# First stage of a two-block transformer kernel: x loaded by two queues, the norm's weights loaded as one row and spread by TensorE, one norm chain for all tokens, projection by halves of the contraction

## What is computed

```python
def rmsnorm(x, g):
    xf = x.astype(jnp.float32)
    y = xf * lax.rsqrt(jnp.mean(xf * xf, axis=-1, keepdims=True) + EPS)
    return (y * g.astype(jnp.float32)).astype(x.dtype)

# first_block, cut
n = rmsnorm(h, g_mix[l])          # x: (1, 256, 1024), g_mix: (1, 1024)
proj = n @ w_in[l]                # convolution, queries, three sets of keys and values, gates
# ... convolution mixer, sparse attention with three branches, w_o, residual
# ... rmsnorm with g_ffn, gated feed-forward, residual, rmsnorm with g_final
# second_block: norm, projections, differential attention, gated linear attention,
# pooling, w_out, residual, norm, gated feed-forward, residual
```

## Time and profile before

| | us |
|---|---|
| median of 3 runs (lowest, highest) | 803.18 (801.69, 803.35) |
| the profiled execution | 801.18 |
| its span | 799.4 |
| TensorE matmuls busy in it | 762.5 (95%) |
| VectorE busy | 519.9 (65%) |
| ScalarE busy | 396.4 (50%) |
| GpSimd busy | 74.0 (9%) |

### The profile page before, as it was taken

One profiled execution on the slowest core, in us unless ns is written; L12 is line 12 of the kernel. 1 busy time (PEld: TensorE's weight loads), 2 busy tenths in 40 slices (PEclk: granted clock), 3 DMA queues, 4 the chain that ended last, 5 costly groups with the idle time before them and its releaser, 6 DMA issues.

```text
span 799.4 us, 13826 instructions
## 1 busy us (share of the span) xinstructions
PE 762.5 (95%) x5693; PEld 717.9 (90%) x5693; DVE 519.9 (65%) x886; ACT 396.4 (50%) x711; POOL 74.0 (9%) x106
## 2 busy tenths in 40 slices
PE   2999999999999998999999998998889999999998
PEld 2999999989989988999899987997769999889996
DVE  5666465765655768776456648687887777447662
ACT  5356655455554445455344536468455454444441
POOL 8000000023022001000000003301500000000000
PEclk9999999999999999999999999999999999999999
DMA  9887636234334565565665553643344665665521
GB/s 289 227 263 238 163 69 191 98 107 139 126 107 135 173 193 184 164 207 191 188 199 164 206 182 99 198 143 121 104 144 121 210 209 170 202 209 160 194 72 52
DMA packets 108414, 132.12 MB, mean 165 GB/s; under 512 B 4267, under 2 KB 97513, under 8 KB 108352
## 3 DMA queue, kind: packets, MB, share of 16 engines
q1 hardware_dynamic: 106048, 126.56, 49.7%
q0 software_dynamic: 2304, 4.68, 2.5%
HBM read 129.39 MB, written 1.84 MB: 164 GB/s over the span
## 4 chain that ended last, share of the span: by engine, by line
PE 58%; DVE 7%; ACT 2%; issue 2%; POOL 1%; POOLq 0%; DVEq 0%
PE B L1421 34%; PE B L1438 23%; DVE LO L892 3%; ACT HI L508 1%; POOL SGC L463 1%; DVE AL L898 0%; PE B L1445 0%; PE B L1576 0%; DVE TMP L1337 0%; ACT SGC L820 0%; DVE NW L908 0%; DVE ST L1164 0%; ACT AH L512 0%; DVE SGC L1262 0%; DVE SM L1254 0%
## 5 line engine op out<-in xcount | busy, mean ns | idle before, releaser
L892 DVE TENSOR_TENSOR LO<-RAW,HI 128x1024 fp32r<-128x1024 f32 x240 | 282.5, 1212 | 105.0 <-ACT HI L508 104.5
L1421 PE MATMUL B<-AH,HI 128*128 128x256 f32 x1200 | 345.0, 288 | 5.9 <-DVE SGC L1179 1.9
L1421 PE MATMUL B<-AL,HI 128*128 128x256 f32 x1200 | 340.5, 284 | 0.0
L1421 PE MATMUL B<-AH,LO 128*128 128x256 f32 x1200 | 340.5, 284 | 0.0
L508 ACT ACTIVATE HI<-RAW 128x1024 fp32r<-128x1024 f32 x240 | 237.7, 1039 | 64.1 <-PE B L1438 59.7
L1421 PEld LDWEIGHTS B<-AH,HI 128*128 128x128 f32 x1200 | 230.7, 192 | 8.9 <-DVE SGC L1179 2.3
L1421 PEld LDWEIGHTS B<-AL,HI 128*128 128x128 f32 x1200 | 230.8, 192 | 0.3
L1421 PEld LDWEIGHTS B<-AH,LO 128*128 128x128 f32 x1200 | 230.6, 192 | 0.0
L1438 PE MATMUL B<-HI,AH 128*128 128x512 f32 (+1 forms) x400 | 140.7, 352 | 6.4 <-DVE AL L1353 3.8
L1438 PE MATMUL B<-LO,AH 128*128 128x512 f32 (+1 forms) x400 | 139.4, 348 | 0.0
L1438 PE MATMUL B<-HI,AL 128*128 128x512 f32 (+1 forms) x400 | 139.4, 348 | 0.0
(11 more groups left out here) (274 smaller groups left out, 591.2 us busy)
## 6 DMA issues: line engine op xcount, KB each, us to landing
RAW<-in_w_in SPq DMA_DIRECT2D x30, 1024.0 KB, 5.6
RAW<-in_w_gate SPq DMA_DIRECT2D x22, 1024.0 KB, 5.3
RAW<-in_w_up SPq DMA_DIRECT2D x22, 1024.0 KB, 5.3
RAW<-in_w_down SPq DMA_DIRECT2D x22, 1024.0 KB, 5.0
RAW<-in_w_in SPq DMA_DIRECT2D x9, 512.0 KB, 5.8
RAW<-in_w_attn_out SPq DMA_DIRECT2D x4, 1024.0 KB, 5.1
RAW<-in_w_o SPq DMA_DIRECT2D x4, 1024.0 KB, 5.0
RAW<-in_w_out SPq DMA_DIRECT2D x4, 1024.0 KB, 5.0
```

The lines of the kernel that those rows point to most:

```text
L892: e.tensor_tensor(pieces(LO, NSPL, i, k), pieces(RAW, NRAW, i, k), pieces(HI, NSPL, i, k), ALU.subtract).then_inc(split_lo, 1)
L1421: x = e.matmul(dst, w[:, t, c0:c0 + n], a, start=(t == 0 and k == 0), stop=(t == nk - 1 and k == 2))
```

## The change

- x: SyncE issues the two halves of token tile 0, ScalarE the two halves of token tile 1, each on its own queue.
- Unit 0 is loaded in two halves by chunks (0 to 3, 4 to 7), the first with a semaphore of its own. Behind it, SyncE waits until all of token tile 1 is there before it issues units 1, 2, 3 and so on.
- g_mix is loaded as one row of 4 KB into partition 0. TensorE multiplies it with a row of ones, in two matmuls of 512 columns, which leaves it spread over 128 partitions in banks 2 and 3. For this `ones` is set earlier (behind the identity matrix).
- VectorE multiplies x by the spread weights first (four instructions of 512 columns, for t, then h), then runs one Newton chain for both token tiles (two values per partition), and then scales tile 0 in place by its factor. ScalarE scales tile 1.
- The pieces are turned by halves of the contraction: TensorE turns half 0 of both tiles, runs the first half of the keys' contraction for c = 0, turns half 1 of both tiles, runs the first half for c = 1, and then the second halves for c = 0 and c = 1. The number of matmuls and transposes is the same. On ScalarE both `hi(0, 1)` and `hi(1)` stand behind the last turned piece, on VectorE `lo(0, 1)` behind it.
- g_ffn is loaded later (once x is scaled), the sums of squares write their unused output to `QK` instead of `TOK`, and the semaphores of nine small loads are merged into two, with which the later waits are for more than they were.

```diff
         @block.sync
-            for t in range(2):
-                for h in range(2):
-                    e.dma_start(X[:, t, halves(h)], A["x"][0, t * 128:(t + 1) * 128, halves(h)]).then_inc(x_in[2 * t + h], 16)
+            for h in range(2):
+                e.dma_start(X[:, 0, halves(h)], A["x"][0, 0:128, halves(h)]).then_inc(x_in[h], 16)
             for i, (src, nk, n, _, _) in enumerate(units):
...
-                if len(src.shape) == 4:
+                if i == 0:
+                    e.dma_start(dst[:, 0:4, :], src[:, 0:4, :]).then_inc(unit0_in, 16)
+                    e.dma_start(dst[:, 4:8, :], src[:, 4:8, :]).then_inc(raw_in[0], 16)
+                    for h in range(2):
+                        e.wait_ge(x_in[2 + h], 16)
+                elif len(src.shape) == 4:
...
         @block.gpsimd
-            gain(0, A["g_mix"][0, :])
+            e.dma_start(GB[0:1, 0, :], A["g_mix"]).then_inc(gain_in[0], 16)
             e.memset(ident[:, :], 0.0).then_inc(setup, 1)
             e.wait_ge(setup, 1)
             e.affine_select(out=ident[:, :], in_=ident[:, :], compare_op=ALU.not_equal, fill=1.0, base=0,
                             pattern=[[-1, 128]], channel_multiplier=1).then_inc(setup, 1)
+            e.memset(ones[:, :], 1.0).then_inc(setup, 1)
...
             e.wait_ge(scaled_sb, 4)
             gain(0, A["g_final"])
+            gain(1, A["g_ffn"][0, :])
...
         @block.scalar
+            for h in range(2):
+                e.dma_start(X[:, 1, halves(h)], A["x"][0, 128:256, halves(h)]).then_inc(x_in[2 + h], 16)
...
-                    squares(2 * t, X[:, t, :], TOK[:, t, :], h)
-            turned(0, B[5], 0, 0)
-            turned(1, B[6], 4, 0)
+                    squares(2 * t, X[:, t, :], QK[:, t, :], h)
             hi(0, 0)
-            turned(2, B[5], 0, 1)
+
+            def scaled(h):
+                e.wait_ge(gained_sb, 3 + h)
+                e.activation(TOK[:, 1, halves(h)], TOK[:, 1, halves(h)], ACT.Copy, scale=ST[:, 7:8]).then_inc(scaled_act, 1)
+
+            e.wait_ge(root0_sb, 1)
+            for h in range(2):
+                scaled(h)
+                for t in range(2):
+                    turned(2 * h + t, B[5 + t], 4 * h, t)
             hi(0, 1)
-            turned(3, B[6], 4, 1)
             hi(1)
...
         @block.vector
+            e.wait_ge(gain_pe, 1)
             for t in range(2):
-                e.wait_ge(squares_sb, 2 * t + 2)
-                own.step(e.scalar_tensor_tensor(ST[:, 4 + t:5 + t], ST[:, 2 * t:2 * t + 1], EPS,
-                                                ST[:, 2 * t + 1:2 * t + 2], ALU.add, ALU.add))
-                own.step(rsqrt(ST[:, 6 + t:7 + t], ST[:, 4 + t:5 + t], 1))
-                own.wait()
-                if t == 0:
-                    e.wait_ge(gain_in[0], 16)
                 for h in range(2):
-                    c = halves(h)
-                    e.scalar_tensor_tensor(TOK[:, t, c], X[:, t, c], ST[:, 6 + t:7 + t], GB[:, 0, c], ALU.mult,
-                                           ALU.mult).then_inc(scaled_sb, 1)
-            turned(0, B[5], 0, 0)
-            turned(1, B[6], 4, 0)
-            turned(2, B[5], 0, 1)
+                    e.wait_ge(x_in[2 * t + h], 16)
+                    e.tensor_tensor(TOK[:, t, halves(h)], X[:, t, halves(h)], B[2 + h][:, :], ALU.mult).then_inc(gained_sb, 1)
+            e.wait_ge(squares_sb, 4)
+            own.step(e.scalar_tensor_tensor(ST[:, 4:6], ST[:, 0:4:2], EPS, ST[:, 1:4:2], ALU.add, ALU.add))
+            rsqrt(ST[:, 6:8], ST[:, 4:6], 2).then_inc(root0_sb, 1)
+            e.wait_ge(root0_sb, 1)
+            for h in range(2):
+                e.wait_ge(gained_sb, 1 + h)
+                e.tensor_scalar(TOK[:, 0, halves(h)], TOK[:, 0, halves(h)], ST[:, 6:7], None, ALU.mult).then_inc(scaled_sb, 2)
             lo(0, 0)
-            turned(3, B[6], 4, 1)
+            for h in range(2):
+                for t in range(2):
+                    turned(2 * h + t, B[5 + t], 4 * h, t)
             lo(0, 1)
             lo(1)
...
         @block.tensor
-            e.wait_ge(setup, IDENT)
-            for t in range(2):
-                for h in range(2):
-                    e.wait_ge(scaled_sb, 2 * t + h + 1)
-                    turn(2 * t + h, TOK[:, t, halves(h)], 5 + h)
+            e.wait_ge(setup, ONE)
+            e.wait_ge(gain_in[0], 16)
+            for h in range(2):
+                take(2 + h, gained_sb, 4)
+                x = e.matmul(B[2 + h][:, :], ones[0:1, :], GB[0:1, 0, halves(h)], start=True, stop=True)
+            x.then_inc(gain_pe, 1)
+
+            def turns(h):
+                e.wait_ge(scaled_sb, 2 * h + 2)
+                turn(2 * h, TOK[:, 0, halves(h)], 5)
+                e.wait_ge(scaled_act, h + 1)
+                turn(2 * h + 1, TOK[:, 1, halves(h)], 6)
...
-            for c in range(2):
-                keys(U_KEYS, 0, c)
+            turns(0)
+            for part in range(2):
+                for c in range(2):
+                    if part == 0:
+                        take(c, keys_sb, c + 1)
+                    x = stationary(U_KEYS, 128 * c, B[c][:, 0:S], 0, c == 0, (turn_lo, 2, 4) if c == 0 else None, part=part)
+                    if part == 1:
+                        x.then_inc(keys_pe, 1)
+                    elif c == 0:
+                        turns(1)
```

54 lines of the change are left out of this document (26 added, 28 removed).

## The result

The changed kernel takes 805.54 us (median of 7 runs, 804.4 to 807.59) against 801.92 for the kernel before beside it: a ratio of 1.0034, 95% interval 1.0018 to 1.0051. The ratio is taken over all runs and not from the two medians, which by themselves lie 3.6 us apart. By it the change is slower by 0.34%, some 2.7 us. The profiled execution took 805.88, its span is 804.1.

What follows compares the result with a forecast made beforehand. TensorE, gated by the end of the keys' matmuls: T of 8.3 plus 18.7 gives 27.0 against 26.6, 0.4 us later; added to the median 803.18 this makes 803.6 us, range 801.1 to 806.5.

Steps and rivals of the forecast that it cites:

- keys through after 28.6: Sign of being wrong: last matmul of the keys through before 25 or after 28.6, where 27.0 was forecast.
- no wait for `lo` or a late unit before 60 us: Signs of being wrong: TensorE's half-us wait for `lo` absent, or a later unit's DMA waited for between 27 and 60.
- T: First stage: the moment at which the spread weights stand in PSUM, forecast at 8.3 us.
- the row: g_mix's load on GpSimd's queue: issued at 1.31, taken to land 3.3 us later, at 4.6; bounds 4.1 and 6.3.
- the row is late: Rival: row lands 5.0 us after issue, T is 10.0, total +2.1, 805.3; chance 0.1.
- The second queue for x: Loading x: ScalarE's two issues (0.9 us) lie under x's flight and were costed at nothing.
- The faster loading of x, by itself, buys nothing: Loading x: all of x is there by T, and VectorE's wait for the weights stands first in its stream.
- The wait for the remainder of unit 0: TensorE before the keys' second halves: remainder ready at T + 16.0, first halves done at T + 15.5, wait 0.5 us.
- The rival that it stays low: Rival: TensorE's pace stays 0.21 us per matmul in the keys' second halves; near 806.2, at most 806.6; chance 0.2.
- spreading: TensorE's two float32 matmuls of 512 columns on the row, at the lower clock level: 3.6 us.
- products: VectorE's x times spread weights, four instructions of 512 columns: 2.5 us.
- one chain: Newton chain for two values as for one, 2.1 us; root at T + 4.6, second chain gone from the path.

Runs made afterwards that it cites:

- after_again: The changed kernel, unchanged, profiled and timed once more: 805.44 us, ratio 1.0038 to the kernel before.
- e1: Changed kernel with the g_mix row issued by SyncE ahead of x instead of by GpSimd: 801.07 us, ratio 0.9989 to the kernel before.
- e7: Changed kernel with all four pieces of x issued by SyncE, the row still by GpSimd: 804.19 us, ratio 1.0015 to the kernel before.
- e6: Kernel before with only token tile 1 of x issued by ScalarE's queue: 802.39 us, ratio 0.9995 to the kernel before.
- e2: Changed kernel with unit 0's second half rounded and its remainder taken earlier, ahead of the last turned pieces: 804.24 us, ratio 1.0019 to the kernel before.
- e12: Changed kernel with both the row by SyncE ahead of x and unit 0's second half early: 800.81 us, ratio 0.9974 to the kernel before.
- e3: As e2, but all four pieces turned before the keys, which then run unbroken: 806.58 us, ratio 1.0040 to the kernel before.
- e4: Changed kernel with g_mix again broadcast by its own 512 KB GpSimd DMA, without row and spreading matmuls: 802.92 us, ratio 0.9999 to the kernel before.
- e8: e12 plus 12 and 5 unread float32 matmuls filling TensorE's idle stretches: 797.61 us, ratio 0.9934 to the kernel before.
- e9: e12 with squares and products in the order in which x and the spread weights arrive: 800.43 us, ratio 0.9964 to the kernel before.
- e11: Kernel before plus only unread filler matmuls on TensorE (16, 12 and 5) around the first transposes: 801.89 us, ratio 0.9980 to the kernel before.

## Why the prediction was right, and where it was off

The account held: what moves the end of the keys moves the end of the program. The range (801.1 to 806.5) holds the time, 805.54, but it does so by its width: the forecast was 803.6 with a range of its own from 802.2 to 804.8, and the time lies above that (+0.4 was forecast for the end of the keys, +2.05 came). By the prediction's own sign, keys through after 28.6, the forecast was wrong, if narrowly (28.64, and 29.28 in after_again); the two other signs, no wait for `lo` or a late unit before 60 us, did not come. The likeliest single outcome was "same" with 0.47; slower by over 0.2%, which came, had 0.38. What held is the account behind T: the distances there are close to their forecasts.

| from T to | predicted | after | e1 |
|---|---|---|---|
| root | 4.6 | 4.6 | 4.7 |
| first turn | 5.3 | 5.2 | 5.4 |
| keys' first matmul | 8.6 | 8.7 | 8.9 |
| keys through | 18.7 | 18.5 | 18.7 |

(after: 14.69, 15.33, 18.80 and 28.64, less 10.12; e1: 11.02, 11.69, 15.16 and 25.03, less 6.29. In after_again the last is 19.1.)

**The step that failed is the row.** The prediction bounded its landing by 2.8 and 5.0 us from issue, "so I take a value nearer the lower end, 3.3". The trace has 4.98, the upper bound. The argument for the lower end was that GpSimd's small loads had stood behind the 512 KB broadcast and behind each other. With the broadcast gone and the row first in the queue, it took as long as they did. The near row was of the same queue and the same microseconds, the far one (a piece of x, by SyncE) of another queue. By SyncE, and ahead of x, the same row took 1.69. T came out at 10.12 instead of 8.3. Between the +0.4 of the forecast and the +2.05 of the trace lie this 1.8 and -0.2 behind T. The case that came true is the rival "the row is late", which had T = 10.0, +2.1 and 805.3, and a chance of 0.1 where it deserved the larger one.

The Trainium skill, DMA: Bandwidth & Descriptors, "SWDGE vs HWDGE vs iDMA", says that a queue fed from SyncE or ScalarE is set up faster than one fed by GpSimd. The runs agree in the direction, 1.69 against 4.98 us, with the place of the row changed too. The section "Anatomy of one DMA" of the same page of the Trainium skill, which the prediction cited with 2.0 us for a small GpSimd load, pointed the wrong way for this moment: in the DMA views of the first 7 us no row of that queue shows less than 4.0. Later it comes nearer. A load of 0.5 KB that GpSimd issues near 16 us lands after 2.5 us in the changed kernel, and after 5.9 in the kernel before, where the 512 KB of g_ffn stand ahead of it in the queue (DMA view of 11 to 19 us; changed kernel, then before):

```profile
REL<-in_rel_bias POOLq DMA_DIRECT2D x1, 0.5 KB, 2.5
```

```profile
REL<-in_rel_bias POOLq DMA_DIRECT2D x1, 0.5 KB, 5.9
```

That fits the prediction's argument that a backlog makes these loads slower. What the argument missed is that in the first microseconds they are slow without one; why isn't shown.

**The second queue for x.** It was costed at nothing and cost 0.8 us, through a path that the prediction did not look at: not the transfer of x, but the row on GpSimd's queue beside two others (e7, one trace against four). "The faster loading of x, by itself, buys nothing" was right for the changed kernel, and nearly so for the kernel before, where 2.7 us at x became 0.8 at the keys (e6). The Trainium skill's rule on the same page, "Issuing engines are not separate DMA queues", has it that a second issuing engine saves only the time of issuing. This case differs in both directions: in the kernel before, the last piece of x came 2.7 us sooner by two queues, where SyncE saved 1.0 us of issuing (1.81 to 0.84), and in the changed kernel the row came 0.8 later.

**The wait for the remainder of unit 0** was foreseen in its place, for its reason, and mis-sized: 0.5 against 1.52. The difference is the pace. It rose during the second turn, so c = 1 was done at 23.98, T + 13.9, not at T + 15.5, and TensorE waited longer for a remainder that came at 25.6 (T + 15.5, forecast T + 16.0). The two errors cancel in the sum, which is luck: the 18.7 behind T was right as a whole and not in these two terms. e2 shows that the order costs 1.0 us.

**The pace.** The rival that it stays low fell: the second halves ran at 0.12. When it rises isn't fixed: between some 2.7 us (changed kernel, during the second turn) and some 5.5 us (e7) after the keys' first matmul, with the same instructions. Transposes between the matmuls did not keep it from rising. The Trainium skill, TensorE: Matmul & The Clock Gate, "Part 4: PE-mode transpose", says that transposes don't count as busy for the clock as matmuls do. e7 could be read so; in e1 and the changed kernel the pace rose while transposes ran. These runs don't settle it, as none had transposes alone for longer than the 1.94 us of a burst.

**Also right:** spreading 3.75 against 3.6, products 2.48 against 2.5, one chain 2.2 against 2.1, and the later units in time, with no wait for a transfer between 27 and 60 us.

**What stays open.** The wait for a unit near 125 us was 2.2 in both traces of the changed kernel and 1.3 and 1.4 in both of the kernel before, but it was long in e6, e7 and e12 too, short in e2 and e3, as before in e4, and 1.5 in e1, e8, e9 and e11; no edit goes with it. And the number of stretches at the lower level late in the program (one in each trace of the kernel before and in e4 and e8, two in e1 and e3, three in each of the changed kernel and in e2, e6, e9 and e11, four in e7 and e12) follows no edit that I can name. What TensorE did before is seen: in after_again each of the three stands right behind a lull, the last behind 3.40 us with 1.17 busy. But the kernel before has a lull of 1.17 in 3.40 us near 580 too, and no fall behind it. Each costs some 1.5 us where TensorE is the bound. They would explain why the last column of the table scatters by about 1 us around the fourth.

## What to carry to other kernels

The first small load that everything waits for belongs on a hardware queue, ahead of the bulk, not on GpSimd's: here 3.3 us for moving one line. When a bound for an unseen transfer is taken from two rows, the row of the same queue in the same microseconds counts for more than one of another queue or another moment: on one queue 0.5 KB took 2.5 us near 16 us, where 4 KB had taken 4.98 at the start. And where an engine's first work comes in bursts, a few matmuls that nobody reads may be worth as much as the reordering: 2.1 us here, beside some 2.3 for the repaired change.

## What I had not expected of the hardware

- A 4 KB row is usable 4.98 us after its issue by GpSimd beside two busy hardware queues, 4.15 beside one, and 1.69 (1.5 to 2.3 in other runs) by SyncE ahead of x and half a us earlier.
- By GpSimd's queue beside two hardware queues, 512 KB (6.29 us) cost only 1.3 us more than 4 KB (4.98); beside one it was 3.4 more (7.54 against 4.15).
- Float32 matmuls of 128 columns on constants raise TensorE's pace before the data are there (e11), and it survives gaps of 0.8 us (e8), 2.4 us ahead of the first turn and 0.96 ahead of the second (e11); eight transposes took 1.09 to 1.35 us instead of 1.97.
- The granted clock of the windows (PEclk) reads 1.00 in the first 20 us, although the matmuls there follow at 0.21 us; in the later stretches near 500, 550 and 585 us it falls below 1.00.
